# Five output projections in half-row chunks 512 columns wide, and the last jobs of two attention mixers beside the first two chunks

## The reference

```
qkv = x @ w_qkv + b_qkv            # 16 query heads, 4 key/value heads, 64 wide
scores = q @ k.T / 8               # blocks of 128 queries, own and previous block of keys, window 128
probs = softmax([scores, sink])[..., :-1]
h = h + rmsnorm((probs @ v) @ w_o + b_o, g)
```

## Time and profile before

| | us |
|---|---|
| median of 3 runs | 3320.06 (3319.93 to 3322.04) |
| profiled execution | 3318.66 |
| its span, first to last instruction | 3316.8 |

### The profile page before, as it was taken

How to read it: one execution, slowest core, us unless ns; L and a number is a source line. 1 busy time by engine, 2 the same in 40 slices (tenths; PEclk the granted TensorE clock), 3 DMA queues, 4 the chain that set the end, 5 groups by cost and what they waited for, 6 DMA issues and landing times.

```text
span 3316.8 us, 43927 instructions
## 1 busy us (share of the span) xinstructions
PE 2943.9 (89%) x17510; PEld 2574.8 (78%) x17510; DVE 1969.6 (59%) x2350; ACT 1427.1 (43%) x1782; POOL 33.4 (1%) x19
## 2 busy tenths in 40 slices
PE   8987999998499999666887799998799999999998
PEld 6876787878388788665876688887688787988887
DVE  5665666663756665556455566666566665655565
ACT  4454445443344544442221344545444544444444
POOL 0000000000000000000000000000000000000000
PEclk9998999998699999786998799999899999999999
DMA  8643555644056565330000465664365564752663
GB/s 241 199 127 99 175 177 176 196 131 154 0 178 190 165 192 179 112 91 1 1 1 21 122 189 170 188 183 127 102 196 169 174 194 126 210 162 94 188 189 95
DMA packets 625086, 471.49 MB, mean 142 GB/s; under 512 B 41441, under 2 KB 592737, under 8 KB 624948
## 3 DMA queue, kind: packets, MB, share of 16 engines
q1 hardware_dynamic: 620292, 460.01, 46.1%
q10 hardware_dynamic: 4656, 9.56, 0.9%
HBM read 466.63 MB, written 1.84 MB: 141 GB/s over the span
## 4 chain that ended last, share of the span: by engine, by line
PE 77%; DVE 13%; ACT 4%; issue 2%; PEldq 1%; DMA 1%; DVEq 1%; ACTq 0%; SPq 0%; PEld 0%
PE pair_bank L371 25%; PE pair_bank L372 13%; PE pair_bank L519 11%; PE out_banks L384 6%; PE out_banks L386 6%; PE out_banks L385 6%; PE out_banks L519 3%; DVE low L306 1%; DVE mix L1947 1%; PE pair_bank L1788 1%; ACT high L302 1%; PEldq L228 1%; PE pair_bank L1801 1%; DVE h L654 1%; DVEq L228 1%
## 5 line engine op out<-in xcount | busy, mean ns | idle before, releaser
L306 DVE TENSOR_TENSOR low<-raw,high 128x3072 fp32r<-128x3072 f32 (+3 forms) x328 | 935.2, 2851 | 787.1 <-ACT high L302 785.2
L371 PE MATMUL pair_bank<-x_parts,high 128*128 128x512 f32 x3520 | 1240.5, 394 | 10.9 <-DVE x_parts L702 8.4
L372 PE MATMUL pair_bank<-x_parts,low 128*128 128x256 f32 x3520 | 987.4, 281 | 0.0
L302 ACT ACTIVATE high<-raw 128x3072 fp32r<-128x3072 f32 (+3 forms) x328 | 774.5, 2361 | 341.7 <-PE out_banks L386 193.4
L371 PEld LDWEIGHTS pair_bank<-x_parts,high 128*128 128x128 f32 x3520 | 662.0, 188 | 166.9 <-issue 14.1
L372 PEld LDWEIGHTS pair_bank<-x_parts,low 128*128 128x128 f32 x3520 | 668.2, 190 | 9.2
L411 ACT ACTIVATE sq_scratch<-pair_bank 128x512 f32<-128x512 f32 x220 | 131.7, 599 | 585.1 <-PE pair_bank L372 585.1
L384 PE MATMUL out_banks<-high,hid_h 128*128 128x512 f32 x880 | 348.5, 396 | 4.0 <-DVE hid_l L447 4.0
L385 PE MATMUL out_banks<-low,hid_h 128*128 128x512 f32 x880 | 348.0, 395 | 0.0
L386 PE MATMUL out_banks<-high,hid_l 128*128 128x512 f32 x880 | 347.9, 395 | 0.0
L519 PE MATMUL pair_bank<-x_parts,high 128*128 128x256 f32 x1216 | 234.2, 295 | 40.5 <-DVEq L228 32.0
(11 more groups left out here) (350 smaller groups left out, 3121.8 us busy)
## 6 DMA issues: line engine op xcount, KB each, us to landing
raw<-in_ffn_w_in_dram SPq DMA_DIRECT2D x352, 512.0 KB
raw<-in_ffn_w_out_dram SPq DMA_DIRECT2D x176, 512.0 KB
raw<-in_ffn_w_dram SPq DMA_DIRECT2D x132, 512.0 KB
raw<-in_w_in_dram SPq DMA_DIRECT2D x32, 1024.0 KB
raw<-in_gla_w_in_dram SPq DMA_DIRECT2D x12, 1024.0 KB
raw<-in_rwkv_w_rkv_dram SPq DMA_DIRECT2D x12, 1024.0 KB
raw<-in_swa_w_qkv_dram SPq DMA_DIRECT2D x10, 1024.0 KB
raw<-in_swa_w_o_dram SPq DMA_DIRECT2D x8, 1024.0 KB
```

What stands on the lines that cost most here:

```text
L302: nc.scalar.activation(high[u % SPLIT][:, lo:w], raw[u % RAW][:, lo:w], ACT.Copy).then_inc(high_ready, count)
L306: nc.vector.tensor_tensor(low[u % SPLIT][:, lo:w], raw[u % RAW][:, lo:w], high[u % SPLIT][:, lo:w].bitcast(F32), ALU.subtract).then_inc(we ...
L371: nc.tensor.matmul(o, H[:, w], x_parts[:, k, :], start=(k == 0), stop=False)
L372: last = nc.tensor.matmul(o[:, 0:SEQ], L[:, w], xh[:, k, :], start=False, stop=(k == KB - 1))
```

## The change

The four row-block chunks of an output projection become four chunks of half the rows and half the columns. `half_rows` gives them in the order (rows 0 to 511, columns 0 to 511), (rows 0 to 511, columns 512 to 1023), and then the lower rows likewise. A chunk has again 2048 words per partition. Each group is 4 x 3 matmuls of 512 columns into a whole bank; the lower rows go on in the sum of the upper ones. All five output projections use it: both SWA, GLA, RWKV, and `w_out_2`.

```
+def half_rows(w):
+    v = w.rearrange("(k p) n -> p k n", p=P)
+    return [Chunk(KB // 2, D // 2, [(0, v[:, k0:k0 + KB // 2, h * D // 2:(h + 1) * D // 2])], k0=k0, half=h)
+            for k0 in (0, KB // 2) for h in range(2)]
...
-                            o = out_bank[2 * t + c // 2][:, (c % 2) * CH:(c % 2) * CH + n]
-                        groups.append((o, [(xx[k][:, t * P:(t + 1) * P], W[:, k * n:(k + 1) * n])
+                            o = out_bank[2 * t + chunk.half][:, :]
+                        groups.append((o, [(xx[chunk.k0 + k][:, t * P:(t + 1) * P], W[:, k * n:(k + 1) * n])
...
-                        if c == 0 and x == 0 and j % 3 == 0:
+                        if (c == 0 or chunk.k0 > 0 and chunk.half == 0) and x == 0 and j % 3 == 0:
...
-                        last = nc.tensor.matmul(o, a, b, start=(j == 0), stop=(j == len(terms) - 1))
+                        last = nc.tensor.matmul(o, a, b, start=(j == 0 and (whole or chunk.k0 == 0)),
+                                                stop=(j == len(terms) - 1 and (whole or chunk.k0 > 0)))
```

The SWA projections and `w_out_2` get `flows=True`, with which all engines pass the barrier ahead of them, and x is awaited by row block instead:

```
-            if tile_early(then):
+            if tile_early(then) or then.flows:
                 return True
...
+    def attended_wait(e, pe, k):
+        a0 = stages[2].first_job
+        if k == 0:
+            pe.wait_ge(e.named("swa_max"), a0 + 7)
+        pe.wait_ge(e.named("swa_low"), a0 + 2 * (k // 2) + 2)
```

The last steps of the SWA jobs move into the projection. On PE (`beside_pe`, after the group named):

```
+        if st.dest == "out":
+            if (c, half) == (0, 0):
+                turn(5)
+                pe.wait_ge(e.named("swa_max"), a0 + 8)
+            elif (c, half) == (0, 1):
+                values(5)
+                turn(6)
+            elif (c, half) == (1, 0):
+                values(6)
+                turn(7)
+            elif (c, half) == (1, 1):
+                values(7)
...
         elif (c, half) == (6, 1):
             scores(6)
-            scores(7)
             turn(4)
             values(4)
-            turn(5)
-            values(5)
...
+            scores(7)
```

More of the change, by code:

```diff
@@ L1155, in out_high @@
             last.then_inc(e.named("swa_high"), 1)
-        if c == 2:
+        if st.dest == "out":
+            if c == 0:
+                copy(5)
+                exps(7)
+                out_high(5)
+            elif c == 1:
+                copy(6)
+                out_high(6)
+                copy(7)
+                out_high(7)
+        elif c == 2:
             exps(0)
@@ L1225, in out_low @@
             last.then_inc(e.named("swa_low"), 1)
-        if (c, emptied) == (0, False):
+        if st.dest == "out":
+            if (c, emptied) == (0, False):
+                normed(6)
+                out_low(4)
+                normed(7)
+            elif (c, emptied) == (0, True):
+                out_low(5)
+            elif (c, emptied) == (1, False):
+                out_low(6)
+                out_low(7)
+        elif (c, emptied) == (0, False):
             e.link(dve, v_.tensor_scalar(negsinks(e.mix), sinks(e.mix), -1.0, None, ALU.mult))
@@ L1266, in swa @@
                     beside_act=beside_act, beside_dve=beside_dve),
-              Stage("proj", chunks=columns(io["swa_w_o"][j], 0, D), feature_major=False, dest="out", evac=None, x=attended_x),
+              Stage("proj", chunks=half_rows(io["swa_w_o"][j]), feature_major=False, dest="out", evac=None, x=attended_x,
+                    x_wait=attended_wait, flows=True, beside_pe=beside_pe, beside_act=beside_act, beside_dve=beside_dve),
               Stage("post", gain=post_gain, norm=True, scale=1.0, bias=bo)]
@@ L1460, in gla @@
               Stage("turn", kb=KB),
-              Stage("proj", chunks=columns(io["gla_w_o"][0], 0, D), feature_major=False, dest="out", evac=None),
+              Stage("proj", chunks=half_rows(io["gla_w_o"][0]), feature_major=False, dest="out", evac=None),
               Stage("post", gain=post_gain, norm=True, scale=1.0, bias=None)]
@@ L2028, in rwkv @@
               Stage("turn", kb=KB, src=result),
-              Stage("proj", chunks=columns(io["rwkv_w_o"][0], 0, D), feature_major=False, dest="out", evac=None),
+              Stage("proj", chunks=half_rows(io["rwkv_w_o"][0]), feature_major=False, dest="out", evac=None),
               Stage("post", gain=post_gain, norm=True, scale=1.0, bias=None)]
@@ L2689, in back @@
     def back(name, **more):
-        return Stage("proj", chunks=columns(io[name][0], 0, D), feature_major=False, **more)
+        w = io[name][0]
+        return Stage("proj", chunks=half_rows(w) if more["dest"] == "out" else columns(w, 0, D), feature_major=False, **more)
     stages = [Stage("pre", gain=io["mix_norm_2"][0], columns=io["c_gains"][13]), Stage("turn", kb=KB),
@@ L2698, in hybrid @@
                    beside_dve=branch_b_dve),
-              back("w_out_2", dest="out", evac=None, x=lambda e: (tails(e.high), tails(e.low)), x_wait=merged_wait),
+              back("w_out_2", dest="out", evac=None, x=lambda e: (tails(e.high), tails(e.low)), x_wait=merged_wait,
+                   flows=True, beside_pe=out_pe, beside_act=out_act, beside_dve=out_dve),
               Stage("post", gain=None, norm=False, scale=1.0, bias=None)]
```

58 lines of the change are left out of this document (23 added, 35 removed).

## The result

The changed kernel takes 3289.22 us (median; 3286.5 to 3291.0) against 3319.99 us (3317.34 to 3322.04) for the kernel before on the same chip. The ratio is 0.991, with a 95% interval of 0.9896 to 0.9924: 0.9% faster, 30.8 us. The forecast was 3288 and 32.0 us. The profiled execution took 3289.34 us with a span of 3287.5; before it was 3318.66 and 3316.8, so the span lost 29.3. One run of experiment 2 (4936.67 us, clock 0.55) was a slow one and is left out; all others were fast.

A forecast was written before the change was run, and what follows sets the result against it. TensorE was taken as the bound, with 77% of the chain; 15.4 + 13.0 (SWA) + 2.6 (hybrid) + 1.0 (width) = 32.0 us saved gave 3286.7 for the profiled execution and 3288 for the median, range 3280 to 3304.

The forecast's parts named there:

- What bounds: Whole kernel: TensorE carries 77% of the chain; a change pays where PE works less or the chain leaves it.
- SWA tail, 15.4 and 13.0: Jobs before the SWA output projection: running them between its chunks saves 15.4 us in layer 0, 13.0 in layer 3.
- chunk 4: no gain: SWA layers: evacuating chunk 4 before job 3's mask gains nothing, a loss of 0.3 us; bounds -1.5 to +2.
- earlier evacuation of chunk 6: SWA layer 0: this evacuation no longer waits for job 5's mask, ending at 277.8 instead of 279.7 us.
- The low part of job 4: SWA layer 0 projection: job 5's values wait for this VectorE step, ending at 293.3, and start at 293.4 us.
- Width: Output projections: 512-wide matmuls at 0.233 us each save 0.5 us each in GLA and RWKV, 1.0 together.
- Rival B: Five output projections: 512 columns cost 0.213 us, gaining about 8.5 us more, 3279.5 us; chance 0.05.
- C: SWA projection: clock stays at 1.2 GHz until job 7's values, 11 us per layer, 3310 (half way 3299); chance 0.08.
- D: SWA projection: clock low to its end, 20 us lost per layer, 3328 us; chance 0.03.
- E, the hand-overs: SWA projection: ScalarE and VectorE queue order holds each step, saving only 8 us per layer, 3300 us; chance 0.10.
- F, no overlap: SWA projection: the first wait or a barrier holds chunk 0 to the end, 3313 to 3320 us; chance 0.02.
- Hybrid, 2.6: Hybrid block: output projection starts before the last merge, whose transposes stand between chunk 0's halves, saving 2.6 us.

The follow-up runs named there:

- experiment 2: Changed kernel with each 512-wide output-projection matmul issued as two of 256 columns, order and overlap kept: 3292.73 us, ratio 0.9925.
- 12: Changed kernel with jobs 5 to 7 run in series before the SWA projection, behind a barrier: 3307.57 us, ratio 0.9974.
- 1: Kernel before with the half-row, 512-wide chunks in all five output projections and nothing moved: 3319.71 us, ratio 1.0007.
- 3: Changed kernel with job 3's mask back ahead of the evacuation of chunk 4: 3286.58 us, ratio 0.9903.
- 4: Changed kernel with job 5's mask back ahead of the evacuation of chunk 6: 3291.16 us, ratio 0.9919.
- experiment 6: Changed kernel with job 3's exponentials on ScalarE behind the split of chunk 6 instead of ahead: 3283.69 us, ratio 0.9903.
- Experiment 7: Changed kernel with job 5's exponentials ahead of job 4's high part, and job 4's low part earlier on VectorE: 3286.31 us, ratio 0.9905.
- 5: Changed kernel with 26 unused transposes filling PE's gaps before chunk 0 of the SWA projection, to hold the clock up: 3286.91 us, ratio 0.9906.
- 8: Changed kernel with job 3's exponentials later and job 4's low part earlier, both together: 3277.32 us, ratio 0.988.
- 9: Changed kernel itself run again, on a third chip: 3287.0 us, ratio 0.991.
- 10: Changed kernel with job 3's exponentials later and job 4's low part earlier, repeated on a third chip: 3278.68 us, ratio 0.9884.
- 11: Changed kernel with the hybrid mixer's last merge back in the branch stage, behind the barrier: 3291.16 us, ratio 0.992.

## Why the prediction was right, step by step

- **What bounds.** Right. The time came from the tail, where PE was idle and slow in turn, and not from the projections' own work (12 shows 22 us of overlap, 1 shows no measurable gain by width).
- **SWA tail, 15.4 and 13.0.** Measured 15.1 and 13.2. In layer 0 the placement of single steps held to 0.8 us (the transposes of job 5, earlier than placed), the rest to 0.5. The term "chunk 4: no gain" is confirmed by 3, and the "earlier evacuation of chunk 6" by 4 (1.55 and 2.1). In layer 3 the agreement is partly luck. The forecast took over that chunk 6 starts 1.0 us later there than in layer 0, which in the kernel before came mostly from chunk 5 (5.26 us at a clock of 0.50, and 4.44 at 0.62 in layer 0). In the changed kernel chunk 5 runs at full clock, and the lost time is another: 1.5 us in chunk 6 (experiment 6).
- **The low part of job 4.** The mechanism (values of 5 wait for it) was right and its place too (293.4 against 293.80), but as a wait of PE it was forecast at 0.5 and measured at 1.46, since the second half of chunk 0 was done at 292.3 instead of 292.9 and the low part was 0.4 late. Experiment 7 gives back 1.2 per layer. The end moved little because the next wait (job 7's low part, 0.3 forecast, 0.16 measured) shrank for it.
- **Width.** 512 columns at full clock cost 0.23 (0.2275 to 0.233), as the FFN's rows said, and at half clock 0.427, the lower bound of the forecast. The 1.0 for GLA and RWKV was locally 0.9 (25.78 to 24.87) and 1.3 (25.84 to 24.54), so too small by 1.2: the price of 0.233 came from 12 matmuls, and 60 in a row of the hybrid block take 13.67 us, 0.228 each. But RWKV's projection starts 708.00 us into its stretch instead of 706.65, with no edit ahead of it, and so its gain doesn't reach the end. A load's trigger is the split of four chunks before, not three as the prediction has it; the term stays 0. Rival B (0.213) is refuted. The figure of the Trainium skill ("TensorE: Matmul & The Clock Gate", Back-to-back issue gap), 216 ns, is given there for the isolated gap of one matmul, and the same section gives about 131 ns for a sustained stream with weight loads. Stretches of 12 and more such matmuls lie at 228 to 233 here, above both; the measurement decides.
- **Rivals C and D, the clock.** Refuted: 1.00 from 287 on, and 1.00 in both stretches after 288. Even the cold start matters little here (5: 0.8 us and nothing). The Trainium skill's warning cited there ("TensorE: Matmul & The Clock Gate", A second HAM failure mode: psum-queue depth-cycling), short pauses between groups that make the clock swing, is not borne out by this stretch: halves of 12 matmuls with pauses of up to 1.46 us between them stayed at 1.00 from 288 to 315.
- **E, the hand-overs.** Refuted as a bound (PE waits 1.62 us inside the projection, not the 7 that E takes back), though its own sign, PE idle over 1 us ahead of chunk 1, is there. It is the right name for what was left: 8 gets some 3.3 us more per layer out of nothing but ACT's and DVE's order. My forecast had 2.49 us of this in it (the transposes of job 3 at 267.1) and took it as given.
- **F, no overlap.** Refuted by the rows. Its price was right at its cheap end: the kernel of 12 is 8.75 us faster than the kernel before on its chip (3307.57 against 3316.32), 6.0 without the hybrid's 2.75, and F said 6.6 (3313). The earlier evacuations and the width pay by themselves.
- **Hybrid, 2.6.** Locally 2.75. The stage shows 1.05, because the changed kernel lost 1.7 earlier in it, at places with no edit (the first 48 matmuls in 7.59 us, not 6.13, and 528 in 64.92, not 63.62; part of it comes back between).
- **Sum.** 32.0 forecast, 29.3 in the profiled span, 30.8 in the medians. The difference of 2.7 is not in a step of the working: the SWA terms are off by 0.1 together. It is in stages that have no edit (+1.9 in one FFN, +1.7 early in the hybrid block, +1.35 ahead of RWKV's projection, -1.8 in GLA, +0.8 in the rest: +4.0), which the sum took as unchanged. That the total is off by 2.7 and not by 4.0 is luck: the width term was 1.2 too small. The 30.8 of the medians lie closer still, over other runs than the profiled one.

## What to carry to other kernels

When a chain of small jobs through three engines stands ahead of a long stage on one of them, find what that stage's first part really needs, and put the jobs between its parts: 22 of 30 us came from that. Moving a step earlier on one queue pays only if nothing on the consumer's other queues is pushed behind it (3 against 4), so after the large move read the waits again and reorder the helper engines' lists; here two such edits gave another 8 us. Before a difference between two profiles is put down to an edit, find the first place where they part and read the clock there: in two segments here it was 1.3 and 1.5 us of what looked like the edit's. A gain of 1 us per stage in a kernel of 3.3 ms is to be read in its own rows, and not in the time.

## What was not expected of the hardware

The untouched stages do not take the same time in all kernels. GLA takes about 209.8 us (after; experiments 3, 5, 6, 8, 9 and 10) or 211.5 to 213.9 (before, 1, 2, 4, 7, 11 and 12), though its width is the same in all but the kernel before and 2; the granted clock is the only other difference found in the rows that were compared. The same 48 matmuls, in a place without an edit, in the kernel before and in the kernel after:
```profile
809.21:817.32 8.11, 8.09 (x48) 7.99 (x48) 2.29 (x1) 1.91 (x1) 0.00 (x0) 0.66 0.33 98
```
```profile
793.90:800.20 6.30, 6.29 (x48) 6.21 (x48) 2.29 (x1) 1.91 (x1) 0.00 (x0) 0.86 0.08 21
```
8.11 us at a mean clock of 0.66 against 6.30 at 0.86: 1.8. The FFN behind RWKV goes the other way, 196.2 against 198.1; five microseconds near its start (5.5 and 5.1 us into it), before and after:
```profile
1885.00:1890.00 5.00, 4.74 (x27) 3.80 (x26) 2.35 (x4) 1.41 (x2) 2.60 (x1) 1.00 0.36 106
```
```profile
1867.00:1872.00 5.00, 5.00 (x22) 4.28 (x21) 2.75 (x6) 1.52 (x3) 3.03 (x1) 0.68 0.32 104
```
PE does the same kind of work in both, and the second row is the slower one though PE is busy throughout it (the first has a pause of 0.26). The moment at which the clock rises differs by up to 2 us between executions. It may hang on the moment at which the stage is reached, so that any edit upstream shifts it; no run here tests that, and what decides it is left open. It puts a floor of 2 to 4 us per stage under what a change can be said to have done by its segment in one profile. Layer 3 of the changed kernel has a stretch of 5.4 us at 0.69, where full speed takes 3.9, in both of its profiles: in chunk 6 where the layer takes 111.70, and from job 1's transposes to its values where it takes 112.51.
